# State stores issued earlier on the load queue, and the token sums of the multiplied-out MLP products moved from GpSimd to VectorE

## The chip, the cores and the metric

One core of a Trainium2 chip runs the whole program. The metric is the device time in microseconds of one execution; smaller is better. TensorE (PE) multiplies, ScalarE (ACT), VectorE (DVE) and GpSimd (POOL) work on what it needs and makes, and SyncE (SP) issues nearly all transfers from its queue.

## The reference

A two-layer decoder step for 512 prompt tokens and 32 sample tokens (544 columns), in float32, with 1024 features:

```python
for l in range(DEPTH):                       # DEPTH = 2
    h = rmsnorm(x, g_mix[l])
    if l < N_A_LAYERS:                       # layer 0: convolution module
        y, nh = conv_module(h, hist[l], w_pw1[l], b_pw1[l], w_dw[l], b_dw[l],
                            g_cln[l], b_cln[l], w_pw2[l], b_pw2[l])
        new_hist.append(nh)                  # the last 30 GLU rows: the "state"
    else:                                    # layer 1: latent attention
        q_lat, q_pe = mla_queries(h, cos, sin, w_dq[j], g_q[j], w_uq[j], w_qr[j], w_uk)
        ...
    x = x + y
    x = x + squared_relu_mlp(rmsnorm(x, g_ffn[l]), w_up[l], w_down[l])   # relu(h @ w_up)**2 @ w_down
```

The state of the prompt is 30 rows, that of each of the 8 sample sequences 30 rows.

## The kernel before

Features lie on the 128 partitions, tokens along the free dimension, so x is 8 chunks of 128x544. Each float32 factor is split into a high and a low part, and a product is three passes (high x high, low x high, high x low). A **unit** is one 128-column piece of a weight matrix: ACT copies its high part (`high`, line 679, tile wh), POOL subtracts to make its low part (`low`, line 524, tile wl), PE multiplies (`product`, line 1522, 48 matmuls of 272 columns in two halves). Two units come from one loaded **block** of 128x8x256 (1 MB, tile raw, line 466); there are two places for blocks, so the load of block n waits until the low parts of block n-2 are made. There are four half-places for weight parts, so the high part of unit u waits for the product of u-2, and two places in PSUM, so product u waits until DVE has read product u-2 (semaphore `freed`).

Every engine runs its own list in the order in which it is written; semaphores tie the lists together. The order around the change is:

- Second pointwise product of the convolution module: blocks 8 to 11 (`w_pw2`), 8 units. After each, `new_x` adds the product to x (DVE, line 1189), makes the next input's high part (ACT, line 687, xh), low part (DVE, line 1014, xl) and the square (ACT, line 693), and DVE adds it up (line 1026, acc). On ACT the call `ahead(u)`, which makes the high part of unit u+2, stands ahead of the rest of `new_x(u)`.
- The two state outputs, `o_convp` (from ext) and `o_convs` (from exs), are stored from the SP queue once the last gated rows are there (`u_out`). ACT waits for both stores (`s_out`) ahead of the MLP, since the MLP's tiles lie over ext and exs.
- MLP of a layer: 8 up products (`ML`), the first of which is followed by the matmuls of the column sums (`sums`, line 1532), ACT's square root (`root_of`, line 698) and DVE's `reciprocal` (line 1033). After it DVE applies the scale and the relu (`relu`, line 1200), ACT squares (`squared`, lines 786, 787), and DVE makes the low part (line 1012). In the same 8 steps the inputs of seven-factor products are prepared, in four groups k: ACT scales two chunks of x (`scaled_x`, line 776, bb), four subtractions make T1, T3, T2 and T4N (`token_sums`, lines 533 to 538, tt), ACT takes their high parts (`token_high`, line 780, th) and DVE their low parts (`token_low`, line 1213, tl). bb and tt have two places each.
- Then 12 pairs of an up block in seven factors (`factor`, line 1647) and a down block (line 1659), and the last down products.

Of the kernel before, what the change touches and what calls it, by code (L numbers as in the profile page):

```python
# [18 lines left out]
ALU = mybir.AluOpType  # L19
# [159 lines left out]
def decoder_program(nc, xT, hist, vecs, cons, rope_tab, rows0, page_table, cache_ckv, cache_kpe, w_pw1, w_pw2, w_up, w_down,  # L179
# [17 lines left out]
    with ExitStack() as ctx:  # L197
# [240 lines left out]
        def _(sp):  # L438
# [37 lines left out]
                         hist.rearrange("p c b t -> p (c b) t")).then_inc(s_hist, 16)  # L476
            sp.dma_start(pt[:, :], page_table).then_inc(s_idx, 16)
            sp.dma_start(r0[:, :], rows0).then_inc(s_idx, 16)
            for n in range(2, MB[0]):
                load(n)  # L480

            sp.wait_ge(u_out, 2 * DC)
            sp.dma_start(o_convp, ext[:, :, NP:NP + HIST]).then_inc(s_out, 16)
            sp.dma_start(o_convs.rearrange("p c b t -> p (c b) t"),
                         exs[:, :, :, NT:NT + HIST].rearrange("p c b t -> p (c b) t")).then_inc(s_out, 16)

            for n in range(MB[0], MB[0] + FB * DC - 2):
                load(n)

            sp.wait_ge(s_out, 32)  # L490
# [27 lines left out]
        def _(pool):  # L518
# [4 lines left out]
                pool.wait_ge(w_hi, u + 1)  # L523
                pf.tensor_tensor(weight(wl, u), weight_raw(u), f32(weight(wh, u)), ALU.subtract).then_inc(w_lo, 1)  # L524

            def token_sums(layer, k):

                n, i = layer * KH + k, k % 2
                pool.wait_ge(t_in, 2 * n + 2)
                if k >= 2:  # L530
                    pool.wait_ge(t_lo, n - 1)
                near, far = bb[:, i, 0, :], bb[:, i, 1, :]
                pf.tensor_tensor(tt[:, i, T1, :], near[:, TB], near[:, TA], ALU.subtract).then_inc(t_sum, 1)
                pf.tensor_tensor(tt[:, i, T3, :], far[:, TB], near[:, TB], ALU.subtract).then_inc(t_sum, 1)
                pool.wait_ge(t_sum, 4 * n + 1)
                pf.tensor_tensor(tt[:, i, T2, :], far[:, TB], tt[:, i, T1, :], ALU.subtract).then_inc(t_sum, 1)
                pool.wait_ge(t_sum, 4 * n + 3)
                pf.tensor_tensor(tt[:, i, T4N, :], far[:, TA], tt[:, i, T2, :], ALU.subtract).then_inc(t_sum, 1)

            def third_sum(layer, q):  # L540

                n = MB[layer] + DC // 2 + 2 * q
# [11 lines left out]

            def mlp(layer):
                for j in range(DC):
                    if 2 <= j < 2 + KH:
                        token_sums(layer, j - 2)
                    low(ML[layer] + j)
                third_sum(layer, 0)  # L560
                for q in range(PAIRS):
                    u = LU[layer] + q * PAIR
                    low(u)
                    low(u + 1)
                    fourth_sum(layer, q)
                    for j in range(2, PAIR):
                        low(u + j)
                    if q + 1 < PAIRS:
                        third_sum(layer, q + 1)
                for j in range(DC):  # L570
                    low(LD[layer] + j)
# [84 lines left out]
        def _(act):  # L656
# [39 lines left out]
            def root_of(dim, e=0, to=None):  # L696
                root_in()
                af.activation(halves(to or rstd[:, :]), SUMS, ACT.Sqrt, bias=eps[:, e:e + 1],
                              scale=1.0 / dim).then_inc(root, 1)
# [64 lines left out]

            for c in range(DC):
                new_x(U_PW2 + c, xh, "g_ffn0")
            root_of(D)

            def scaled_x(layer, g, k):

                n = layer * KH + k
                if k >= 2:
                    act.wait_ge(t_sum, 4 * (n - 1))
                for e in range(2):
                    c = k + e * KH
                    af.activation(bb[:, k % 2, e, :], x[:, c, :], ACT.Copy, scale=V(g, c)).then_inc(t_in, 1)

            def token_high(layer, k):
                act.wait_ge(t_sum, 4 * (layer * KH + k) + 4)
                af.activation(th[:, k, :, :], tt[:, k % 2, :, :], ACT.Copy).then_inc(t_hi, 1)  # L780
# [8 lines left out]
            def mlp(layer, g):  # L789
                for k in range(2):  # L790
                    scaled_x(layer, g, k)
                for j in range(DC):
                    ahead(ML[layer] + j)
                    squared(0, j)
                    if 1 <= j < 1 + KH:
                        token_high(layer, j - 1)
                    if 1 <= j < KH - 1:
                        scaled_x(layer, g, j + 1)
                for q in range(PAIRS):
                    u, n = LU[layer] + q * PAIR, layer * PAIRS + q  # L800
                    f, c = q // (DC // 2) + 1, q % (DC // 2) * 2

                    if n > 0:
                        act.wait_ge(u_read, n)
                    act.wait_ge(mm, u + 1)
                    af.activation(acc[:, TA], factor_out(u, 0), ACT.Copy).then_inc(u_copy, 1)
                    for j in range(FACTORS - 1):
                        ahead(u + j)
                    squared(f, c)
                    ahead(u + FACTORS - 1)  # L810
                    squared(f, c + 1)
                    for j in range(FACTORS, PAIR):
                        ahead(u + j)
# [167 lines left out]
            af.activation(mh[:, :, NP:T], ps[:, 5, 0:NH * NS].rearrange("p (h s) -> p h s", s=NS), ACT.Copy).then_inc(s_hi, 1)  # L981
            for c in range(DC):
                new_x(U_WO + c, xh2, "g_ffn1")
            root_of(D)
            mlp(1, "g_ffn1")
            for c in range(DC):
                u = LD[1] + c
# [8 lines left out]
        def _(dve):  # L996
# [33 lines left out]
            def reciprocal(to=None):  # L1030
                root_()
                r = to or rstd[:, :]
                link(df.reciprocal(r, r))
# [159 lines left out]

            for c in range(DC):
                new_x(U_PW2 + c, xl, xh, "g_ffn0", "b_pw2")
            reciprocal()

            def relu(dst, a, scale, sem_=None):

# [7 lines left out]
            def down(u, c):  # L1207
                dve.wait_ge(mm, u + 1)
                df.tensor_tensor(halves(x[:, c, :]), acc_of(u), halves(x[:, c, :]), ALU.add).then_inc(freed, 1)

            def token_low(layer, k):
                dve.wait_ge(t_hi, layer * KH + k + 1)
# [37 lines left out]
                squared_low(f, c)  # L1250

            def mlp(layer, nsrc):
                for j in range(DC):
                    u = ML[layer] + j
                    dve.wait_ge(mm, u + 1)
                    relu(halves((t0, t1)[j % 2][:, :]), acc_of(u), halves(rstd[:, :]), src)
                    dve.wait_ge(src, nsrc + j + 1)
                    dve.sem_inc(freed, 1)
                    squared_low(0, j)
                    if 2 <= j < 2 + KH:  # L1260
                        token_low(layer, j - 2)
                    if j == DC - 3:
                        first_sums(layer, 0)
                for q in range(PAIRS):
                    up_pair(layer, q, nsrc)
                    if q + 1 < PAIRS:
                        first_sums(layer, q + 1)
                    squared_low(q // (DC // 2) + 1, q % (DC // 2) * 2 + 1)
                    for j in range(2):
                        down(LU[layer] + q * PAIR + FACTORS + 2 * j + 1, q % (DC // 2) * 2 + j)  # L1270
# [212 lines left out]
            df.tensor_tensor(ml[:, :, NP:T], ps[:, 5, 0:NH * NS].rearrange("p (h s) -> p h s", s=NS), f32(mh[:, :, NP:T]), ALU.subtract).then_inc(s_lo, 1)  # L1483
            for c in range(DC):
                new_x(U_WO + c, xl2, xh2, "g_ffn1")
            reciprocal()
            mlp(1, FB * DC + 3 + NH // 2)
            for c in range(DC):
                u = LD[1] + c
# [499 lines left out]
```

## Time and profile before

| | us |
|---|---|
| median of three runs (lowest, highest) | 1467.7 (1467.69, 1469.43) |
| the profiled execution | 1465.78 |
| its span in the trace | 1464.0 |
| PE busy in the span | 1386.7 (95%) |
| DVE, ACT, POOL busy | 816.4, 606.9, 764.1 |
| mean granted TensorE clock | 0.979 of full |
| PE's share of the chain that ended last | 85% |
| share of `DMA raw<-w_up` in that chain | 2% |

Times within the trace are microseconds from the start of its span. The profiled execution lies 1.9 us under the median, so differences are taken in the trace and then applied to the median. A busy PE is no PE at its peak: matmuls overlap, so the distance from one product to the next is the measure.

### The profile page before, as it was taken

The page shows a single profiled execution, that of the slowest core. Times are in us where ns is not written, and L with a number is a line of the kernel's source. Part 1 is how long each engine was busy: PE and PEld are TensorE (multiplying, and loading weights), DVE is VectorE, ACT ScalarE, POOL GpSimd, SP SyncE. Part 2 cuts the span into 40 slices and gives each one's busy share as a digit, 9 for nine tenths or more (in the row PEclk, how much of TensorE's full clock was granted, in tenths as well). Part 3 has the DMA queues.
Part 4 walks back from the last instruction along what each step waited for, and adds up shares of the span by engine and source line. Part 5 has one row for each costly group of instructions (what it writes and reads, how often), then busy time and mean ns, then how long its engine had stood idle before and what let it go on. Part 6 is the DMA issues. An engine that isn't in the chain of part 4 may idle for free.

```text
span 1464.0 us, 28984 instructions
## 1 busy us (share of the span) xinstructions
PE 1386.7 (95%) x12444; PEld 1289.4 (88%) x12444; DVE 816.4 (56%) x1199; ACT 606.9 (41%) x1030; POOL 764.1 (52%) x541
## 2 busy tenths in 40 slices
PE   6999969799999999998899999999999999999995
PEld 5787759789999999998899967677998999999995
DVE  5658775455454454468456655655455545545435
ACT  5212243444444344345456644443354443444432
POOL 3422203468788888333323354340357887887732
PEclk9999979899999999999999999999999999999998
DMA  8312109323322322522111376662122322322221
GB/s 193 87 30 59 60 1 63 86 84 104 99 87 87 109 94 87 189 87 74 55 33 33 114 280 256 264 249 78 58 87 71 103 87 89 109 92 88 87 87 61
DMA packets 132143, 148.69 MB, mean 102 GB/s; under 512 B 22768, under 2 KB 123248, under 8 KB 127792
## 3 DMA queue, kind: packets, MB, share of 16 engines
q1 hardware_dynamic: 124848, 104.90, 25.3%
q0 software_dynamic: 7168, 41.95, 7.6%
q8 instruction: 98, 1.61, 0.5%
q14 instruction: 29, 0.24, 0.0%
HBM read 142.81 MB, written 4.03 MB: 100 GB/s over the span
## 4 chain that ended last, share of the span: by engine, by line
PE 85%; DVE 5%; POOL 3%; ACT 3%; DMA 2%; issue 1%; DVEq 0%; SPq 0%; ACTq 0%; POOLq 0%
PE ps L1522 27%; PE ps L1659 20%; PE ps L1647 17%; PE ps L1790 5%; PE ps L1564 3%; PE ps L1830 3%; POOL wl L524 2%; PE ps L1879 2%; DMA raw<-w_up 2%; ACT wh L679 1%; PE ps L1725 1%; PE ps L1860 1%; DVE xl L1014 1%; PE ps L1888 1%; PE ps L1584 0%
## 5 line engine op out<-in xcount | busy, mean ns | idle before, releaser
L524 POOL TENSOR_TENSOR wl<-raw,wh 128x512 fp32r<-128x512 f32 (+2 forms) x253 | 443.8, 1756 | 402.9 <-ACT wh L679 402.4
L679 ACT ACTIVATE wh<-raw 128x512 fp32r<-128x512 f32 (+2 forms) x253 | 192.6, 762 | 389.3 <-PE ps L1522 200.7
L524 POOL TENSOR_TENSOR wl<-wuv,wh 128x512 fp32r<-128x512 f32 x104 | 134.8, 1308 | 92.0 <-ACT wh L679 92.0
L1522 PE MATMUL ps<-xh,wh 128*128 128x272 f32 x704 | 152.6, 299 | 30.6 <-POOL wl L524 17.9
L1659 PE MATMUL ps<-mh,wh 128*128 128x272 f32 x768 | 158.6, 288 | 0.0
L1659 PE MATMUL ps<-mh,wl 128*128 128x272 f32 x768 | 158.6, 288 | 0.0
L1659 PE MATMUL ps<-ml,wh 128*128 128x272 f32 x768 | 158.3, 288 | 0.0
L1522 PEld LDWEIGHTS ps<-xh,wh 128*128 128x128 f32 x704 | 113.2, 194 | 42.8 <-POOL wl L524 31.0
L1522 PE MATMUL ps<-xl,wh 128*128 128x272 f32 x704 | 147.8, 292 | 0.0
L1522 PE MATMUL ps<-xh,wl 128*128 128x272 f32 x704 | 147.8, 293 | 0.0
L1659 PEld LDWEIGHTS ps<-ml,wh 128*128 128x128 f32 x768 | 120.4, 188 | 0.0
L1659 PEld LDWEIGHTS ps<-mh,wh 128*128 128x128 f32 x768 | 120.3, 188 | 0.0
L1659 PEld LDWEIGHTS ps<-mh,wl 128*128 128x128 f32 x768 | 119.9, 189 | 0.0
L1522 PE MATMUL ps<-mh,wh 128*128 128x272 f32 x544 | 113.6, 290 | 5.5 <-POOL wl L524 3.1
L679 ACT ACTIVATE wh<-wuv 128x512 fp32r<-128x512 f32 x104 | 65.4, 630 | 116.5 <-DVE wuv L1224 79.2
L1522 PEld LDWEIGHTS ps<-xl,wh 128*128 128x128 f32 x704 | 113.4, 193 | 0.0
L1522 PEld LDWEIGHTS ps<-xh,wl 128*128 128x128 f32 x704 | 112.9, 194 | 0.0
L1522 PE MATMUL ps<-mh,wl 128*128 128x272 f32 x544 | 112.8, 289 | 0.0
L1522 PE MATMUL ps<-ml,wh 128*128 128x272 f32 x544 | 112.7, 289 | 0.0
L1647 PE MATMUL ps<-th,wl 128*128 128x272 f32 x384 | 110.8, 289 | 0.0
L1647 PE MATMUL ps<-tl,wh 128*128 128x272 f32 x384 | 110.6, 288 | 0.0
L1647 PE MATMUL ps<-th,wh 128*128 128x272 f32 x384 | 110.6, 288 | 0.0
(284 smaller groups left out, 3080.2 us busy)
## 6 DMA issues: line engine op xcount, KB each, us to landing
raw<-w_up SPq DMA_DIRECT2D x32, 1024.0 KB, 5.4
raw<-w_down SPq DMA_DIRECT2D x32, 1024.0 KB, 5.1
raw<-w_pw SPq DMA_DIRECT2D x16, 512.0 KB, 5.1
raw<-w_pw SPq DMA_DIRECT2D x4, 1024.0 KB, 5.1
raw<-w_o SPq DMA_DIRECT2D x4, 1024.0 KB, 5.1
raw<-w_dq SPq DMA_DIRECT2D x3, 1024.0 KB, 5.3
raw<-w_uq SPq DMA_DIRECT2D x4, 768.0 KB, 4.4
x<-xT SPq DMA_DIRECT2D x4, 544.0 KB, 7.3
```

Of the source, the lines that this page charges most:

```text
L524: pf.tensor_tensor(weight(wl, u), weight_raw(u), f32(weight(wh, u)), ALU.subtract).then_inc(w_lo, 1)
L679: af.activation(weight(wh, u), weight_raw(u), ACT.Copy).then_inc(w_hi, 1)
L1014: df.scalar_tensor_tensor(dst, a, scale, f32(high), ALU.mult, ALU.subtract).then_inc(lo, 1)
L1522: m = tf.matmul(ps[:, 2 * (u % 2) + bank, 0:width], w[:, k, :], a[:, k, part], start=(k == 0 and n == 0), stop=(k == nk - 1 and n == 2))
L1564: m = tf.matmul(ps[SB * j:SB * (j + 1), conv_bank(c) + i, :], diag[part, c % 2, s + j, :], ext[part, c, s + j:s + j + NP], start=(s == 0), ...
L1647: m = tf.matmul(factor_out(u, i), w[:, k, :], part(a, k), start=(k == 0 and n == 0), stop=(k == KH - 1 and n == 2))
L1659: m = tf.matmul(acc_of(u)[:, h, :], w[:, k, :], a[:, k0 + k, h * HALF:(h + 1) * HALF], start=(k0 == 0 and k == 0 and n == 0), stop=(k0 > 0 ...
L1725: m = tf.matmul(out, k[:, c, j * P:(j + 1) * P], w[:, c, :], start=(c == 0 and m_ == 0), stop=(c == KC - 1 and m_ == 2))
L1790: m = tf.transpose(keys_at(n)[:, q * P:(q + 1) * P], a, ident)
L1830: m = tf.matmul(ps[NS * s:NS * (s + 1), 3 + i % 2, :], q, k, start=(c == 0), stop=(c == 2))
L1860: tf.matmul(out[:, c * NS:(c + 1) * NS], oc[:, (SPB * b + k) % SETS, cols], fold_w[:, b % 2, k, :], start=(k == 0), stop=False)
L1879: m = tf.matmul(ps[NS * s:NS * (s + 1), 6, 0:KL], pts[:, q, NS * s:NS * (s + 1)], latents(2 * i + s // 2)[:, r * KL:(r + 1) * KL], start=( ...
```

## The change

Three things are written differently. On SP, the two state stores stand ahead of the load of the third `w_pw2` block (number 10), and not behind the load of the last one (11). The subtractions of `token_sums` are on DVE and not on POOL: groups 0 and 1 ahead of the reciprocal, groups 2 and 3 at the end of steps 0 and 1. On ACT, `scaled_x` of groups 0 and 1 stands ahead of the square root, and `token_high` and the later `scaled_x` come one step sooner. This holds for the MLP of both layers.

```diff
-            for n in range(2, MB[0]):
-                load(n)
-
-            sp.wait_ge(u_out, 2 * DC)
-            sp.dma_start(o_convp, ext[:, :, NP:NP + HIST]).then_inc(s_out, 16)
-            sp.dma_start(o_convs.rearrange("p c b t -> p (c b) t"),
-                         exs[:, :, :, NT:NT + HIST].rearrange("p c b t -> p (c b) t")).then_inc(s_out, 16)
-
-            for n in range(MB[0], MB[0] + FB * DC - 2):
+            for n in range(2, MB[0] + FB * DC - 2):
+                if n == units[U_PW2].block + 2:
+                    sp.wait_ge(u_out, 2 * DC)
+                    sp.dma_start(o_convp, ext[:, :, NP:NP + HIST]).then_inc(s_out, 16)
+                    sp.dma_start(o_convs.rearrange("p c b t -> p (c b) t"),
+                                 exs[:, :, :, NT:NT + HIST].rearrange("p c b t -> p (c b) t")).then_inc(s_out, 16)
                 load(n)
...
             def mlp(layer):                                  # POOL
                 for j in range(DC):
-                    if 2 <= j < 2 + KH:
-                        token_sums(layer, j - 2)
                     low(ML[layer] + j)
...
             def mlp(layer, g):                               # ACT
                 for k in range(2):
                     scaled_x(layer, g, k)
+                root_of(D)
                 for j in range(DC):
                     ahead(ML[layer] + j)
                     squared(0, j)
-                    if 1 <= j < 1 + KH:
-                        token_high(layer, j - 1)
-                    if 1 <= j < KH - 1:
-                        scaled_x(layer, g, j + 1)
+                    if j < KH:
+                        token_high(layer, j)
+                    if j < KH - 2:
+                        scaled_x(layer, g, j + 2)
...
             def mlp(layer, nsrc):                            # DVE
+                for k in range(2):
+                    token_sums(layer, k)
+                reciprocal()
                 for j in range(DC):
                     u = ML[layer] + j
                     dve.wait_ge(mm, u + 1)
...
                     squared_low(0, j)
-                    if 2 <= j < 2 + KH:
-                        token_low(layer, j - 2)
+                    if j < KH:
+                        token_low(layer, j)
+                    if j < KH - 2:
+                        token_sums(layer, j + 2)
                     if j == DC - 3:
                         first_sums(layer, 0)
```

The calls `root_of(D)` and `reciprocal()` that stood behind the loop of `new_x` are gone from there. The four subtractions of a group are the same on DVE as they were on POOL.

The SP queue, from the loads of the second pointwise weights (w_pw 128x8x256) to the first up weights, before:

```order
L466 DMA raw<-w_pw 128x8x256 x4
L483 DMA o_convp<-ext 1024x1x30
L484 DMA o_convs<-exs 8192x1x30
L466 DMA raw<-w_up 128x8x256 x5
```

and in the change:

```order
L466 DMA raw<-w_pw 128x8x256 x2
L482 DMA o_convp<-ext 1024x1x30
L483 DMA o_convs<-exs 8192x1x30
L466 DMA raw<-w_pw 128x8x256 x2
L466 DMA raw<-w_up 128x8x256 x5
```

The stores have moved past two block loads. The larger one is 8192 pieces of 30 numbers (120 bytes).

DVE at the start of the MLP of layer 0, before, from the last sum of squares (acc) to step 2:

```order
L1026 TENSOR_TENSOR acc<-acc,sq 128x544
L1033 RECIPROCAL rstd<-rstd 128x544
L1200 SCALAR_TENSOR_TENSOR t<-ps,rstd 128x544
L1012 TENSOR_TENSOR ml<-sq,mh 128x544
L1200 SCALAR_TENSOR_TENSOR t<-ps,rstd 128x544
L1012 TENSOR_TENSOR ml<-sq,mh 128x544
L1200 SCALAR_TENSOR_TENSOR t<-ps,rstd 128x544
L1012 TENSOR_TENSOR ml<-sq,mh 128x544
L1213 TENSOR_TENSOR tl<-tt,th 128x1088
```

and in the change, where the relu is line 1179, group 0 of the sums stands first and group 1 (its last two rows are shown) next to the reciprocal:

```order
L1200 TENSOR_TENSOR tt<-bb,tt 128x272
L1202 TENSOR_TENSOR tt<-bb,tt 128x272
L1013 RECIPROCAL rstd<-rstd 128x544
L1179 SCALAR_TENSOR_TENSOR t<-ps,rstd 128x544
L992 TENSOR_TENSOR ml<-sq,mh 128x544
L1206 TENSOR_TENSOR tl<-tt,th 128x1088
L1197 TENSOR_TENSOR tt<-bb 128x272
L1198 TENSOR_TENSOR tt<-bb 128x272
L1200 TENSOR_TENSOR tt<-bb,tt 128x272
L1202 TENSOR_TENSOR tt<-bb,tt 128x272
L1179 SCALAR_TENSOR_TENSOR t<-ps,rstd 128x544
```

Between the relu of step 0 and that of step 1 there are now five more instructions; before there was only the low part of ml.

ACT at the same place, before:

```order
L698 ACT_TABLE_LOAD
L698 ACTIVATE rstd<-ps,eps 128x544
L776 ACTIVATE bb<-x,vec 128x544 x4
L679 ACTIVATE wh<-raw 128x1024
L786 ACTIVATE sq<-t 128x544
L787 ACTIVATE mh<-t 128x544
L679 ACTIVATE wh<-raw 128x1024
```

and in the change:

```order
L756 ACTIVATE bb<-x,vec 128x544 x4
L679 ACT_TABLE_LOAD
L679 ACTIVATE rstd<-ps,eps 128x544
L660 ACTIVATE wh<-raw 128x1024
L766 ACTIVATE sq<-t 128x544
L767 ACTIVATE mh<-t 128x544
L760 ACTIVATE th<-tt 128x1088
L756 ACTIVATE bb<-x,vec 128x544 x2
L660 ACTIVATE wh<-raw 128x1024
```

The four scalings stand ahead of the root, and a high part of sums and two scalings now stand between the squares of step 0 and the high part of the weights that step 1 makes.

## Rows read from the trace of the kernel before

**Rows 1.** Chain that ended last, layer 0: start us, us, what
```profile
239.64 24.39 DMA raw<-w_up
...
276.27 0.93 PE ps L1532 x4
...
300.83 25.57 PE ps L1522 x192
326.39 3.62 PE ps L1647 x29
```

**Rows 2.** The same chain, layer 1
```profile
1078.07 0.93 PE ps L1532 x4
...
1128.22 10.52 PE ps L1647 x84
```

**Rows 3.** Timeline of PE: start us, us, what [idle before <- releaser]
```profile
267.60 0.82 PE L1522 MATMUL ps<-xh,wh 128*128 128x272 f32 x2 [7.58 <-POOL wl L524]
...
284.79 0.51 PE L1522 MATMUL ps<-xh,wh 128*128 128x272 f32 x2 [1.61 <-POOL wl L524]
...
300.83 0.82 PE L1522 MATMUL ps<-xh,wh 128*128 128x272 f32 x2 [3.53 <-POOL wl L524]
...
665.22 0.62 PE L1522 MATMUL ps<-mh,wh 128*128 128x272 f32 x2 [1.88 <-DVE ml L1014]
...
694.51 0.52 PE L1522 MATMUL ps<-mh,wh 128*128 128x272 f32 x2 [1.77 <-POOL wl L524]
```

**Rows 4.** Timeline of the SP queue, three stretches
```profile
173.38 0.37 SPq L466 DMA_DIRECT2D raw<-w_pw  x1
...
227.92 1.54 SPq L484 DMA_DIRECT2D o_convs<-exs  x1
239.64 18.70 SPq L466 DMA_DIRECT2D raw<-w_up  x2
```

**Rows 5.** Transfers: issue, count, size, median us from issue to landing
```profile
raw<-w_up SPq DMA_DIRECT2D x32, 1024.0 KB, 5.4
...
o_convs<-exs SPq DMA_DIRECT2D x1, 960.0 KB, 32.6
```

**Rows 6.** Timeline of ACT
```profile
230.06 1.06 ACT L679 ACTIVATE wh<-raw 128x1024 fp32r<-128x1024 f32 x1 [3.35 <-PE ps L1522]
...
287.10 1.10 ACT L780 ACTIVATE th<-tt 128x1088 fp32r<-128x1088 f32 x1
288.10 1.38 ACT L776 ACTIVATE bb<-x,vec 128x544 f32<-128x544 f32 x2
```

**Rows 7.** Timeline of DVE
```profile
173.82 0.24 DVE L1062 SCALAR_TENSOR_TENSOR exs<-t,vec 128x32 f32<-128x32 f32 x1
...
249.90 2.32 DVE L1014 SCALAR_TENSOR_TENSOR xl<-x,vec,xh 128x544 fp32r<-128x544 f32 x1 [1.01 <-ACT xh L687]
252.15 0.71 DVE L1026 TENSOR_TENSOR acc<-acc,sq 128x544 f32<-128x544 f32 x1
254.12 0.78 DVE L1189 SCALAR_TENSOR_TENSOR x<-ps,vec,x 128x544 f32<-128x544 f32 x1 [1.26 <-PE ps L1522]
...
278.04 3.55 DVE L1033 RECIPROCAL rstd<-rstd 128x544 f32<-128x544 f32 x1 [3.97 <-ACT rstd L698]
...
285.24 0.71 DVE L1200 SCALAR_TENSOR_TENSOR t<-ps,rstd 128x544 f32<-128x544 f32 x1
...
293.95 1.29 DVE L1213 TENSOR_TENSOR tl<-tt,th 128x1088 fp32r<-128x1088 f32 x1
...
330.93 0.44 DVE L1235 TENSOR_TENSOR t<-ps,acc 128x272 f32<-128x272 f32 x1 [0.25 <-PE ps L1647]
```

**Rows 8.** Timeline of POOL
```profile
249.24 2.40 POOL L524 TENSOR_TENSOR wl<-raw,wh 128x1024 fp32r<-128x1024 f32 x1 [3.61 <-ACT wh L679]
```

**Rows 9.** Tile tt: engine op xcount: ns min/median/max, first and last start us
```profile
L533 POOL TENSOR_TENSOR tt<-bb x8: 773/782/1262, 279.3 to 1104.5; 128x272 f32<-128x272 f32 x8
```

**Rows 10.** Window 300.8 to 302: us, busy of PE, PEld, DVE, ACT, POOL; PEclk, DMA, GB/s
```profile
300.80:302.00 1.20, 1.17 (x5) 1.18 (x6) 1.20 (x2) 0.00 (x0) 0.00 (x0) 0.50 0.00 0
```

More of the change, by code:

```diff
@@ L524, in low @@
                 pf.tensor_tensor(weight(wl, u), weight_raw(u), f32(weight(wh, u)), ALU.subtract).then_inc(w_lo, 1)
[L526 to L538, printed above, removed]
             def third_sum(layer, q):
@@ L766, in _ @@
                 new_x(U_PW2 + c, xh, "g_ffn0")
-            root_of(D)
             def scaled_x(layer, g, k):
@@ L983, in _ @@
                 new_x(U_WO + c, xh2, "g_ffn1")
-            root_of(D)
             mlp(1, "g_ffn1")
@@ L1195, in _ @@
                 new_x(U_PW2 + c, xl, xh, "g_ffn0", "b_pw2")
-            reciprocal()
             def relu(dst, a, scale, sem_=None):
@@ L1209, in down, with token_sums @@
                 df.tensor_tensor(halves(x[:, c, :]), acc_of(u), halves(x[:, c, :]), ALU.add).then_inc(freed, 1)
+            def token_sums(layer, k):
+                n, i = layer * KH + k, k % 2
+                dve.wait_ge(t_in, 2 * n + 2)
+                if k >= 2:
+                    dve.wait_ge(t_lo, n - 1)
+                near, far = bb[:, i, 0, :], bb[:, i, 1, :]
+                df.tensor_tensor(tt[:, i, T1, :], near[:, TB], near[:, TA], ALU.subtract).then_inc(t_sum, 1)
+                df.tensor_tensor(tt[:, i, T3, :], far[:, TB], near[:, TB], ALU.subtract).then_inc(t_sum, 1)
+                dve.wait_ge(t_sum, 4 * n + 1)
+                df.tensor_tensor(tt[:, i, T2, :], far[:, TB], tt[:, i, T1, :], ALU.subtract).then_inc(t_sum, 1)
+                dve.wait_ge(t_sum, 4 * n + 3)
+                df.tensor_tensor(tt[:, i, T4N, :], far[:, TA], tt[:, i, T2, :], ALU.subtract).then_inc(t_sum, 1)
             def token_low(layer, k):
@@ L1485, in _ @@
                 new_x(U_WO + c, xl2, xh2, "g_ffn1")
-            reciprocal()
             mlp(1, FB * DC + 3 + NH // 2)
```

## The prediction

> **What bounds the kernel now.** I read the page first: PE is busy for 95% of the span and carries 85% of the chain that ended last, so a change pays only where PE stands still or runs at the lower clock, and everything behind such a place moves with it. Then I read the chain around the changed lines. In layer 0 its largest foreign piece is a transfer: the load of the first up block, issued at 239.64, on the chain for 24.39 us [rows 1]; the median load of that kind lands in 5.4 us [rows 5]. The SP queue shows why: the store of o_convs was issued at 227.92 [rows 4] and takes 32.6 us to land [rows 5], until 260.5, and the load stands behind it. PE waits 7.58 us, from 260.02 to 267.60 [rows 3]. It then starts at the lower clock, so that this product with the others up to the sums' matmuls (276.27, [rows 1]) takes 8.67 us, where a product at full clock is 6.0 to 6.05 us (x is written at 254.12 for the product before [rows 7], and PE is done with the next at 260.02 [rows 3]).
>
> The timeline of PE shows two more waits in each layer's up products, both for a low part that POOL made late: 1.61 and 3.53 us in layer 0 [rows 3]. At each of them POOL had one group of token sums in front of the weights' low part, 0.78 us for each of four subtractions [rows 9]. After the wait of 3.53 us the granted clock is 0.50 [rows 10], which is the 1.2 GHz level; the four products from 300.83 take 25.57 us [rows 1], 1.4 us over four at 6.05. Layer 1 is the same: from the sums' matmuls to the first factor 50.15 us [rows 2], against 50.12 in layer 0 [rows 1]. Nothing else in the span depends on the moved lines, so the sum is made from these two stretches.
>
> **Stores moved.** The gated rows of the last chunk are written at 173.82 + 0.24 = 174.1 [rows 7]. Before, the load of the third block was issued at 173.38 [rows 4]; now the stores go at 174.1 and the load right behind them, after their issuing (1.54 us for the large one [rows 4], of which the smaller one's is a part). With the landing of 32.6 us and then 5.4 us for the block behind it [rows 5], the third block is there at about 214. ACT first reads it at 230.06 [rows 6]: 16 us of cover. The stores are down by about 208, and ACT's wait for them stands at 262, so that costs nothing; if the cover were gone, each microsecond of lateness would cost one. The fourth block's load and the first up load are released by low parts that do not move, the latter at 239.64 [rows 4], and it now lands in 5.4 us, at 245. What is next in the line: ACT makes that unit's high part when the product before the last is done, 254.1, POOL its low part until 257.6 (2.40 us [rows 8]), both before PE is free at 260.02. Product one of the MLP starts at 260.07 and not at 267.60, at full clock: ends at 266.1 and not at 276.1. **Gain 10.0 us.** The last input chunk is no new stop: x is written at 260.1, its low part waits on POOL as at 249.90 (2.32 us, ends 4.1 us after x was written at 248.1, a product ahead of 254.12 [rows 7]), so it is there at 264.2, and PE comes to it at 265.3.
>
> **Token sums and the reciprocal.** I count from the sums' matmuls, S (276.27 and 1078.07 now; 266.3 in layer 0 then). The sum of squares ends 4.75 us behind the last x (252.86 less 248.1 [rows 7]), 264.85, S - 1.4 (by layer 1's trace about S - 1.1). A 128x272 subtraction on DVE is not in the trace with both inputs in SBUF. The nearest is 0.44 us with one input in PSUM [rows 7]; the bound from above is POOL's 0.78 [rows 9]; I take 0.43, and with starts that overlap 1.65 us a group. Two groups end at S + 1.9 to S + 2.2; the scalings they need (1.38 us a pair [rows 6]) are done at S - 1.2. The reciprocal now starts at S + 1.8 [rows 1, 7], so it starts 0.1 to 0.4 later, and the first relu, R, at S + 5.7 to S + 6.0, where it was S + 5.4. ACT's scalings ahead of the root fit into its wait. POOL's low part for product 2, with no sums before it, is ready at S + 5.2: product 1 after the sums ends at S + 6.85, product 2 starts at once. The wait of 1.61 us is gone, and the one of 3.53 us in that form.
>
> **What takes their place.** Step 0 now holds a chain. ACT: squares and high part of the sums, from R + 1.86 to R + 2.96 (285.24 to 287.10, 1.10 [rows 6, 7]), scalings to R + 4.24 [rows 6], then the high part of the weights for product 3 until R + 5.2 (1.06 [rows 6]). DVE: low part of the sums 1.29 [rows 7] to R + 4.3, then the four subtractions from R + 4.35. The third would end at R + 5.5; POOL, which asked at R + 5.25, starts its 2.40 us [rows 8] at R + 5.4, and the fourth waits. That DVE with two SBUF inputs stands still until POOL is done is what 249.90 shows: 2.32 us for an instruction that starts 0.66 us behind POOL's at 249.24 and ends 0.58 us after it [rows 7, 8]. So the fourth ends at R + 8.1, relu 1 at R + 8.75. PE has finished product 2 at S + 12.85 and can start product 3 at S + 14.55: a wait of 1.7 us. Step 1 repeats it: relu 2 starts 8.0 us after relu 1, product 4 starts 8.0 after product 3, a wait of 2.0 us. Groups 2 and 3 are then through; step 2 has no subtractions, and PE goes on without waits. The clock: after 1.77 us of waiting PE's first pair of matmuls took 0.52 us, as at full clock, after 1.88 us 0.62 us, a part of it at the lower [rows 3]. I take the lower clock once in a layer, with 1.4 us. From S: 14.55, +8.0, +6.05 +1.4, +3 x 6.05 = 48.1; with R at the early end 47.8. It was 50.1: **gain 2.3 us in layer 0, 2.0 to 2.3 in layer 1**, 4.6 together at the early end, which I take since layer 0's stretch lies there.
>
> The page "SBUF — State Buffer" of the Trainium skill, section "Who interferes with whom", says that a VectorE instruction with two SBUF inputs and a GpSimd instruction that reads SBUF exclude each other for a whole instruction; the trace agrees (2.32 us at 249.90). The page "GPSIMD Engine Reference" of the Trainium skill, section "Engine selection", would put elementwise work on VectorE as about twice as fast: by that alone the move saves and no wait comes back, which is the second case below; by the exclusion it costs two waits a layer.
>
> **Sum.** 10.0 + 4.6 = 14.6 us: span 1464.0 to 1449.4, the profiled execution 1465.8 to 1451.2, the median of 1467.7 to **1453.1**.
>
> **Rivals.**
> - The waits of step 0 and 1 come back without the lower clock, since 1.7 to 2.0 us lies about the 1.77 that did not bring it and the 1.88 that did: 2 x 1.4 less, 1450.3. Chance 0.20.
> - The fourth subtraction gets in ahead of POOL's low part. For: it is 0.04 us behind the third. Against: POOL asks 0.2 us earlier, and waits only for the one that runs. Then only product 3 waits (low part at R + 8.3, 1.3 us), at full clock; each layer ends 3.4 us sooner: 1446.3. If it also cost POOL nothing, 0.6 less in each layer: 1445.1. Chance 0.15.
> - A subtraction takes POOL's 0.78 us. The reciprocal is then 2.9 us later and each of two steps 1.4: 5.7 us a layer, 1464.5. Chance 0.03; in between (0.5 to 0.6 us, or one more lockout of 2.4 us in a step), 1455 to 1459, 0.08.
> - The stores do not hold the load: it would be late without them. For: other transfers share the queue. Against: 32.6 and 24.4 us end within 4 us of each other, and the 32 loads have a median of 5.4. Then 10.0 falls away: 1463.1. Chance 0.02.
> - Slower: the third block comes late. It stands behind 8192 small pieces; if these took 49 us and not 32.6 from 174 on, the block would miss 230.06, and each further microsecond costs one, first out of 14.6. The result turns at 64 us, about twice the row; three times the row, 98 us, gives 1453 + 49 = 1502. For: the stores now run while the convolution reads the same tiles. Against: on the old place they ran beside busy PE, DVE, ACT and POOL, and the products there kept their 6.0 us. Chance 0.03.
>
> **How the numbers follow.** My forecast holds 0.49. Its own range is 1451.5 to 1455. The range of all reaches to the second rival below and to the in-between case above, 1445.5 to 1457, and leaves out about 0.12. What a measurement tells from no change is 0.2%, 2.9 us. Faster by more 0.95, within 0.02, slower 0.03; only the last rival and half-way forms of the third and fourth are not faster.
>
> **What would show it.** In the changed trace the large store lands at about 208 and the first up load in 5 to 6 us; PE has no wait at 260; the sums' matmuls of layer 0 start near 266.3. The span from there to the first factor is 47.8 us in both layers, with two waits of PE of 1.3 to 2.0 us ahead of products 3 and 4, released by DVE's relu, and one of the four subtractions in each of groups 2 and 3 takes 2.4 us or more. The subtractions else take 0.43 us and the reciprocal starts right behind them. I am wrong if the third block's high part is later than 230.1, if DVE is locked out at another place, or if a stage behind takes the shift up.

## The result, and the profile after

| | before | changed |
|---|---|---|
| median, us (lowest to highest, 10 runs each) | 1467.7 (1464.86 to 1472.77) | 1459.8 (1457.2 to 1462.98) |
| ratio to before, 95% interval | | 0.9945 [0.9932, 0.9958] |
| span of the profiled execution, us | 1464.0 | 1458.0 |
| PE busy in the span, us | 1386.7 | 1386.7 |
| sums' matmuls start, layer 0 / layer 1, us | 276.27 / 1078.07 | 276.28 / 1074.49 |

The kernel is faster, by 7.9 us and not by the forecast 14.6: outside the range of 1445.5 to 1457. The last row of the table shows where the sum broke. The sums' matmuls of layer 0 should have come near 266.3, and came where they had been.

The chain that ended last in the changed kernel (start us, us, what), ahead of layer 0's MLP and in it:

```profile
183.00 2.13 PE ps L1561 x47
185.12 5.90 issue
191.02 6.55 PE ps L1561 x110
...
204.93 2.18 PE ps L1574 x4
...
234.12 36.36 PE ps L1519 x288
...
298.93 24.14 PE ps L1519 x192
```

Line 1561 is the depthwise taps, 1519 the product, 1574 the column means behind the taps, and "issue" is time in which PE waited for nothing that the profile shows. The up load that stood on the chain for 24.39 us [rows 1] is gone from it: from 234.12 PE multiplies for 36.36 us without a stop, over the place of the 7.58 us wait [rows 3]. In its place there are 5.90 us in the middle of the taps.

PE's timeline of the changed kernel (start us, us, what [idle before <- releaser]) shows that stop, and the two waits in the up products:

```profile
182.93 2.20 PE L1561 MATMUL ps<-ext,diag 32*32 32x512 f32 x47
191.02 6.43 PE L1561 MATMUL ps<-ext,diag 32*32 32x512 f32 x113 [5.90 <-issue]
...
276.28 1.08 PE L1529 MATMUL ps<-acc,con 128*128 128x272 f32 x4
...
290.95 0.49 PE L1519 MATMUL ps<-xh,wh 128*128 128x272 f32 x2 [1.63 <-DVEq L1254]
...
298.93 0.49 PE L1519 MATMUL ps<-xh,wh 128*128 128x272 f32 x2 [1.77 <-DVEq L1254]
```

The same run of 160 taps in PE's timeline of the kernel before, and the means behind it:

```profile
181.62 5.52 PE L1564 MATMUL ps<-ext,diag 32*32 32x512 f32 x160
...
194.50 2.18 PE L1577 MATMUL ps<-acc,invd 128*128 128x272 f32 x4 [4.76 <-DVEq L1151]
```

Before, the taps took 5.5 us from 181.62. Now they end at 197.45, 14.5 us after their start: 5.9 of stop, and 3.1 more because what follows ran at the lower clock. Two windows of the changed kernel (us, busy of PE, PEld, DVE, ACT, POOL; PEclk, DMA, GB/s) show both:

```profile
185.20:191.00 5.80, 0.00 (x0) 0.00 (x0) 0.85 (x2) 0.00 (x0) 0.00 (x0) 0.81 1.55 49
191.00:194.00 3.00, 2.98 (x61) 1.43 (x66) 0.00 (x0) 0.00 (x0) 0.00 (x0) 0.50 1.56 47
```

In the first every computing engine is all but idle, while the DMA engines show a share of 1.55 and move only 49 GB/s. In the second PEclk is 0.50, the 1.2 GHz level.

What runs there is the large store. The SP queue and the transfers of the changed kernel (issue, count, size, median us to landing), which answer to [rows 4, 5]:

```profile
175.40 0.62 SPq L482 DMA_DIRECT2D o_convp<-ext  x1
176.06 0.68 SPq L483 DMA_DIRECT2D o_convs<-exs  x1
176.78 60.88 SPq L466 DMA_DIRECT2D raw<-w_pw  x2
250.07 54.89 SPq L466 DMA_DIRECT2D raw<-w_up  x5
```

```profile
raw<-w_pw SPq DMA_DIRECT2D x1, 1024.0 KB, 29.7
o_convs<-exs SPq DMA_DIRECT2D x1, 960.0 KB, 28.4
```

The store is on its way from 176.06 to 204.5, over the whole last run of taps; before it began at 227.92 [rows 4], among products.

The page of the changed kernel counts PE's instructions and the packets of the queue q8, the only one with instruction packets of 16 KB (packets, MB, share of 16 engines):

```profile
PE 1386.7 (95%) x12444; PEld 1286.3 (88%) x12444; DVE 830.0 (57%) x1231; ACT 607.2 (42%) x1030; POOL 737.6 (51%) x509
q8 instruction: 98, 1.61, 0.5%
```

PE's 24888 matmuls and weight loads and its 382 recorded waits and drains make 98.7 times 256, for 98 packets. No other engine has as many instructions, so the packets are PE's. Around the stop there is one of them. The window 176.2 to 185.2 holds 4416 packets of q1 and none of q8; the window 185.3 to 185.5 reads:

```profile
q1 hardware_dynamic: 90, 0.01, 171.6%
q8 instruction: 1, 0.02, 79.2%
```

79.2% of 16 engines over 0.2 us is a packet of 2.5 us. It began when PE had already stopped, at 185.12, and PE went on 3.1 us after its end.

DVE's timeline in step 0 of the MLP, layer 0, changed kernel (compare [rows 7]), and POOL's row that collides with it:

```profile
278.44 3.54 DVE L1013 RECIPROCAL rstd<-rstd 128x544 f32<-128x544 f32 x1
...
285.02 1.29 DVE L1206 TENSOR_TENSOR tl<-tt,th 128x1088 fp32r<-128x1088 f32 x1 [0.28 <-ACT th L760]
286.41 0.44 DVE L1197 TENSOR_TENSOR tt<-bb 128x272 f32<-128x272 f32 x1
286.77 0.44 DVE L1198 TENSOR_TENSOR tt<-bb 128x272 f32<-128x272 f32 x1
287.12 0.44 DVE L1200 TENSOR_TENSOR tt<-bb,tt 128x272 f32<-128x272 f32 x1
287.60 2.52 DVE L1202 TENSOR_TENSOR tt<-bb,tt 128x272 f32<-128x272 f32 x1
290.03 0.71 DVE L1179 SCALAR_TENSOR_TENSOR t<-ps,rstd 128x544 f32<-128x544 f32 x1
```

```profile
287.29 2.52 POOL L521 TENSOR_TENSOR wl<-raw,wh 128x1024 fp32r<-128x1024 f32 x1 [5.76 <-ACT wh L660]
```

This is the forecast step by step: three subtractions of 0.44 us, the fourth locked out until POOL is done, the relu behind it, and PE released by that relu (line 1254). The four products from 298.93 take 24.14 us, where they took 25.57 [rows 1]. The clock did not fall; the window that answers to [rows 10] has a PEclk of 1.00:

```profile
298.93:302.00 3.07, 3.07 (x24) 3.07 (x25) 1.72 (x2) 2.99 (x4) 0.00 (x1) 1.00 0.02 5
```

**Account**, in the profiled executions. Up to the sums' matmuls of layer 0: 1.3 us later from the program's start (what stands ahead of the stores comes at 172.88 for 171.57, far ahead of any moved line), 9.1 us later from the last taps (both seen at the means, 194.50 and 204.93), 10.4 us earlier from there on because the up load is there in time: 276.27 stays 276.28. From there to the first factor 46.8 us in each layer (276.28 to 323.07, 1074.49 to 1121.29), for 50.12 and 50.15: 3.3 us gained twice. Between layer 0's first factor and layer 1's sums 0.3: 751.7 (1078.07 less 326.39 [rows 1, 2]) and 751.4. The last sums of squares are multiplied 1.0 us slower, at the lower clock. That makes 6.0, and the span is 6.0 us shorter.

### The profile page after: what moved, and what is told of

Same layout as the page of the kernel before. It is cut to its first block, busy times and chain, and to the rows that moved or that the text cites. A ratio compares the mean times of both kernels' runs of the same rounds, so it can differ in the third digit from the quotient of the medians.

```text
span 1458.0 us, 28984 instructions
## 1 busy us (share of the span) xinstructions
PE 1386.7 (95%) x12444; PEld 1286.3 (88%) x12444; DVE 830.0 (57%) x1231; ACT 607.2 (42%) x1030; POOL 737.6 (51%) x509
## 3 DMA queue, kind: packets, MB, share of 16 engines
q8 instruction: 98, 1.61, 0.5%
## 4 chain that ended last, share of the span: by engine, by line
PE 86%; DVE 8%; ACT 3%; issue 2%; POOL 1%; DMA 0%; DVEq 0%; SPq 0%; ACTq 0%
PE ps L1519 26%; PE ps L1656 20%; PE ps L1644 17%; PE ps L1787 5%; PE ps L1561 4%; PE ps L1827 3%; PE ps L1876 2%; POOL wl L521 1%; DVE rstd L1013 1%; ACT wh L660 1%; PE ps L1722 1%; PE ps L1581 1%; DVE xl L994 1%; DVE tt L1202 1%; PE ps L1885 1%
```

## Experiments

Times are medians; the ratio is to the kernel before on the same chip, with its 95% interval. Its medians were 1466.0 in the first group of runs, 1474.7 in the second and 1466.6 in the third, so groups are compared by their ratios.

**Each half alone.** stores_only is the kernel before with the changed SP list; sums_only is the changed kernel with the old SP list.

> Only the stores are moved; token sums stay on POOL. Theory 1 (PE's instructions come late while the many 120-byte pieces of the state store fill the transfer engines, and this bites in the convolution's tap matmuls, of which PE takes 30 in a microsecond): the stop of PE marked issue, 5.9 us at 185.1 in the changed kernel, is there, the wait of 7.6 us at 260 is gone; 10.0 gained, about 9.1 lost, so the time is 0 to 2 us under before, ratio 0.999. Theory 2 (the stop at 185 was an accident of the profiled execution, or comes from the new order of the MLP): no stop, 10 us gained, ratio 0.993.

> Only the token sums are moved; stores stay behind the last load of the second pointwise weights. If the two parts add up: no stop of PE at 185, the late load with its wait of 7.6 us is there as before, and the stretch from the sums' matmuls to the first factor is 46.6 to 48 us in both layers where it was 50.1: 2.3 to 3.5 us a layer, 5 to 7 us in all, ratio 0.9955. If the gain of the changed kernel came from the stores, ratio 1.000.

Measured: stores_only 1465.65 us, ratio 0.9997 [0.9987, 1.0007]; sums_only 1459.93 us, 0.9958 [0.9943, 0.9973]. The half that should have given 10.0 us gives nothing; the other gives 6.2 us by its ratio and has no stop in the taps, though PE waited 10.28 us for the late up load and not 7.58. PE's timeline of stores_only:

```profile
181.51 2.20 PE L1561 MATMUL ps<-ext,diag 32*32 32x512 f32 x47
191.44 6.94 PE L1561 MATMUL ps<-ext,diag 32*32 32x512 f32 x113 [7.73 <-issue]
```

So the stop belongs to the stores, whatever DVE and POOL do, and it comes behind the same 47th matmul.

**The stores after the taps.** Issued ahead of the fourth block instead, when the last taps are through:

```diff
-                if n == units[U_PW2].block + 2:
-                    sp.wait_ge(u_out, 2 * DC)
+                if n == units[U_PW2].block + 3:
+                    sp.wait_ge(conv_mm, DC)
```

> The changed kernel with the stores one load later (ahead of the fourth block) and waiting for the last tap matmuls (about 187). Theory 1 (late instructions): the store of 28 to 33 us runs while PE does the norm's few matmuls and then products of 0.125 us a matmul; no stop marked issue over 1 us, the taps end where they do before, the stores land by about 220, the fourth block is issued at 227 and lands at once, PE has no wait at 260: 9 us under the changed kernel, about 1451, ratio 0.989. Rival (any small-piece store before 228 takes PE's instructions away, wherever it runs): a stop of some us comes back between 188 and 222, and the gain over the changed kernel is under 4 us.

Measured: 1448.03 us, 0.9875 [0.986, 0.9891]. The taps in PE's timeline:

```profile
182.95 5.52 PE L1561 MATMUL ps<-ext,diag 32*32 32x512 f32 x160
```

The stop and the lower clock are gone, with the same store of the same pieces, which lands in 29.4 us. The sums' matmuls start at 267.12. Against sums_only the stores are now worth 0.83% of 1467.7, 12 us, give or take 3 by the two intervals; the estimate was 10.0. In the traces the sums' matmuls come 9.2 us earlier than before, 10.5 if counted from the start of the last taps (182.95 for 181.62). The price of the late load is itself not fixed: in sums_only the up load issued at 240.15 was on the chain for 27.74 us, in the kernel before for 24.39 [rows 1].

**What of the store does it?** The taps read ext while the stores read ext and exs, so a contended tile was a rival. stores_other_tile sends as many pieces of the same size from xh, which nothing writes at that time; stores_long_pieces sends the same 960 KB in 1024 pieces of 960 bytes. Both also take the small store from xh (line not shown). In both the state outputs hold other numbers, and ACT waits for the stores ahead of its first write of xh.

```diff
-                    sp.dma_start(o_convs.rearrange("p c b t -> p (c b) t"),
-                                 exs[:, :, :, NT:NT + HIST].rearrange("p c b t -> p (c b) t")).then_inc(s_out, 16)
+                    sp.dma_start(o_convs.rearrange("p c b t -> p (c b) t"),    # stores_other_tile
+                                 f32(xh[:, :, :]).rearrange("p c (b t) -> p (c b) t", t=34)[:, 0:DC * NB, 0:HIST]).then_inc(s_out, 16)
+                    sp.dma_start(o_convs.rearrange("p c b t -> p c (b t)"),    # stores_long_pieces
+                                 f32(xh[:, :, 0:NB * HIST])).then_inc(s_out, 16)
```

> The changed kernel, but the stores read the same number of 120-byte pieces from the tile xh, which nobody writes then, and not from ext and exs, so the state outputs hold other numbers; ACT waits for them ahead of the first write of xh. Theory 1 (late instructions): the stop of 5 to 7 us in the tap matmuls stays, time as the changed kernel, ratio 0.9945. Rival (the store and the tap matmuls read the same tile ext and hold each other up): no stop, 9 us faster, ratio 0.988.

> As the kernel that stores from tile xh at the changed place, with the same 960 KB for the large output in 1024 pieces of 960 bytes and not 8192 of 120 (the state outputs hold other numbers). Theory 1 in the form that the number of pieces is what crowds the transfer engines: the large store lands in 3 to 8 us, the stop of PE in the taps is gone or under 1 us, time 8 to 10 us under the changed kernel, ratio about 0.988. Rival (any transfer of this size behind the small prompt store holds PE's instructions up): the stop stays over 3 us, ratio 0.993 or more.

Measured: stores_other_tile 1457.81 us, 0.9951 [0.9935, 0.9966]; stores_long_pieces 1454.84 us, 0.9866 [0.9848, 0.9884]. PE's timeline of the first, then of the second:

```profile
192.65 6.07 PE L1562 MATMUL ps<-ext,diag 32*32 32x512 f32 x113 [7.00 <-issue]
```

```profile
185.18 4.33 PE L1562 MATMUL ps<-ext,diag 32*32 32x512 f32 x113 [1.51 <-issue]
```

The tile does not matter: the stop is as long from another. The pieces do: with an eighth of them the store lands in 8.7 us and the stop is 1.51 us, at the same place. Both are above what was expected (3 to 8 us, and under 1 us). The 1024 pieces of 120 bytes of the small store still ran there, and which of the two stores the 1.51 us belong to was not tested.

**The same pieces, few at a time.** stores_in_eight leaves the stores early in the program (behind the third block's load), still beside the taps, but as eight transfers of 1024 pieces, each issued when the one before it has landed.

```diff
-                if n == units[U_PW2].block + 2:
+                if n == units[U_PW2].block + 3:
...
-                    sp.dma_start(o_convs.rearrange("p c b t -> p (c b) t"),
-                                 exs[:, :, :, NT:NT + HIST].rearrange("p c b t -> p (c b) t")).then_inc(s_out, 16)
+                    for c in range(DC):
+                        if c > 0:
+                            sp.wait_ge(s_hist, 16 * (c + 1))
+                        sp.dma_start(o_convs[:, c, :, :], exs[:, c, :, NT:NT + HIST]).then_inc(s_hist if c < DC - 1 else s_out, 16)
```

> The changed kernel with the third block's load ahead of the stores, and the large store cut into 8 of 1024 pieces each (one feature chunk), each issued when the one before has landed (7 us each by the small store's landing, 174 to about 235), so that never more than 1024 or 2048 pieces are queued. Theory 1a (PE's 16 KB of instructions wait behind the pieces that are already queued): the stop in the taps shrinks to 0 to 2.5 us, ratio 0.987 to 0.989. Theory 1b (small pieces share the engines badly at any queue length): the stop stays 5 us or more, ratio 0.9945.

Measured: 1446.66 us, 0.9865 [0.985, 0.9879]. Its SP queue, its transfers and its taps:

```profile
176.72 40.06 SPq L486 DMA_DIRECT2D o_convs<-exs  x8
```

```profile
o_convs<-exs SPq DMA_DIRECT2D x8, 120.0 KB, 5.0
```

```profile
183.41 5.52 PE L1563 MATMUL ps<-ext,diag 32*32 32x512 f32 x160
```

The eight run beside the taps, from 176.7 on, and PE does not stop. So neither a store beside the taps nor its small pieces do it by themselves, but 8192 of them handed over at once. One thing else differs: the third block's load now goes ahead of the stores and not behind them. The next run takes it out of the question.

**A store among other taps.** If it is PE's supply, the stop must follow the store, and the products must stay free of it. extra_store_mid is stores_after_taps with one more store of 8192 pieces, from xh at 91.34, ahead of an earlier run of taps; the later stores wait for it and overwrite what it writes.

```diff
...
+                if n == 7:
+                    sp.dma_start(o_convs.rearrange("p c b t -> p (c b) t"),
+                                 f32(xh[:, :, :]).rearrange("p c (b t) -> p (c b) t", t=34)[:, 0:DC * NB, 0:HIST]).then_inc(s_hist, 16)
```

> The kernel with the stores behind the last taps, and one more store of 8192 pieces of 120 bytes (from xh into the same output, overwritten later), issued at about 90 us, so that it runs beside products (92 to 107) and the taps of chunk 4 (107 to 115). Theory 1 (PE runs out of instructions in taps): no stop in the products, a stop marked issue of 2 to 8 us in the taps at 107 to 115 or just behind, ratio 3 to 9 us above the kernel with the stores behind the taps. Rival (the stop belongs to the last chunk, its ext data or its place in the program): no stop over 1 us there, time equal to that kernel's 1448.

Measured: 1468.88 us, 0.9958 [0.9943, 0.9973], 0.8% above stores_after_taps by the ratios of their two groups. That is 12 us, where 3 to 9 were expected: the stops are 8.25 us together, and the last taps start 14.15 us later than in stores_after_taps (197.10 for 182.95), since PE also ran at the lower clock behind each stop. PE's timeline in the first run of 224 taps:

```profile
108.44 2.26 PE L1565 MATMUL ps<-ext,diag 32*32 32x512 f32 x54
114.41 6.03 PE L1565 MATMUL ps<-ext,diag 32*32 32x512 f32 x128 [3.70 <-issue]
124.99 3.90 PE L1565 MATMUL ps<-ext,diag 32*32 32x512 f32 x42 [4.55 <-issue]
...
197.10 5.53 PE L1565 MATMUL ps<-ext,diag 32*32 32x512 f32 x160
```

Two windows of it, with the counts of matmuls and weight loads:

```profile
114.30:124.90 10.60, 6.03 (x128) 2.47 (x128) 3.45 (x5) 0.00 (x0) 0.00 (x0) 0.83 0.97 106
124.90:197.05 72.15, 70.87 (x1098) 53.36 (x1098) 47.86 (x67) 16.22 (x23) 19.44 (x9) 0.95 0.15 46
```

The first stop begins at 110.7. The store went out at 91.34 and the next block's load only at 112.12, so no load stood behind the store then.

These rows name the mechanism. The two stops are 128 matmuls and 128 weight loads apart, 256 instructions. From the second stop to the place behind the 47th tap of the last run are 1098 + 47 matmuls and as many loads, 2290 instructions, and the stored trace has 14 waits of PE between them, which the views do not count: 2304, nine times 256. The stops lie on one grid of 256 of PE's own instructions. The page "Runtime: NRT & Kernel Launch" of the Trainium skill, section "Instruction fetch mechanics", says that an engine's instructions are refilled in blocks of 256, 16 KiB, through a DMA queue, and that the cost of crossing from one to the next is "mostly hidden". The trace agrees with the block (98 packets, 1.61 MB in the whole span); that it is hidden does not hold beside 8192 small pieces.

The stored traces give the time of each packet and of each of PE's instructions. Counted with its waits, the instruction behind the 47th tap is number 5057, and number 4801, 256 ahead of it, stands in the run of taps before. A number on the grid is called a border here. The last two runs of the table are shown further below.

| | PE passes 4801, us | q8 packet starts | and takes | PE goes on with 5057 |
|---|---|---|---|---|
| before | 176.27 | 177.49 | 1.05 | 182.84, no stop |
| stores_in_eight | 178.06 | 180.79 | 1.30 | 184.63, no stop |
| stores_long_pieces | 176.13 | 182.73 | 0.96 | 185.18 |
| changed | 177.58 | 185.37 | 2.54 | 191.02 |
| stores_other_tile | 178.12 | 187.98 | 2.72 | 192.65 |
| stores_only | 176.16 | 187.09 | 2.07 | 191.44 |
| sums_behind_relu | 176.04 | 188.55 | 2.78 | 193.56 |
| changed_again | 176.53 | 189.13 | 2.50 | 194.07 |

Without the store beside the taps the packet starts 1.2 to 1.5 us after PE has passed the border before (before, sums_only, stores_after_taps, best and best_again), and PE has its instructions in time. Beside 8192 pieces it starts 7.8 to 12.6 us after, takes twice as long, and PE goes on 2 to 3.1 us behind its end. The later the packet, the longer the stop. In extra_store_mid PE passes the border before the first stop at 98.76, among products, and the packet starts at 109.41.

The same happens at the store's old place, among products. Number 6081, four blocks on, is reached there while the store runs. In the kernel before, PE passed 5825 at 239.82, the packet started at 248.93 and ended at 252.18, and PE came to 6081 at 255.73. In sums_only the packet ended at 253.65, and PE's timeline has a stop at that very instruction:

```profile
256.89 0.52 PE L1522 MATMUL ps<-mh,wl 128*128 128x272 f32 x2 [0.37 <-issue]
```

**The subtractions behind the relu.** sums_behind_relu is the changed kernel, with the subtractions of groups 2 and 3 moved behind the relu of the step after:

```diff
                     dve.sem_inc(freed, 1)
+                    if 1 <= j < KH - 1:
+                        token_sums(layer, j + 1)
                     squared_low(0, j)
                     if j < KH:
                         token_low(layer, j)
-                    if j < KH - 2:
-                        token_sums(layer, j + 2)
```

best has the stores after the taps as well.

> The changed kernel, with the subtractions of groups 2 and 3 on DVE behind the next step's relu and not ahead of it. If PE's waits of 1.63 and 1.77 us ahead of products 3 and 4 come from the relu queued behind the four subtractions and the lockout: relu 1 starts 4.3 us behind relu 0 and not 8.0, PE waits at most 0.7 us ahead of product 3 (for POOL's low part, which ACT starts late) and not at all ahead of product 4; the stretch is 43.9 us and not 46.6 in both layers, 5.4 us together, ratio 0.991. Rival (the low part of the weights is as late as the relu and holds PE by itself): 1 us a layer or less.

> Both later places together: stores behind the last taps, subtractions of groups 2 and 3 behind the relu. If the two do not touch each other: 10 us for the stores and 5.4 us for the subtractions under the changed kernel, 1443 on the scale where before is 1466, ratio 0.984.

Measured: sums_behind_relu 1461.17 us, 0.9895 [0.9873, 0.9918], in spite of a stop of 9.98 us in its taps; best 1449.37 us, 0.9826 [0.9811, 0.9841]. PE's only wait in layer 0's up products of best, then DVE's timeline:

```profile
280.88 0.52 PE L1519 MATMUL ps<-xh,wh 128*128 128x272 f32 x2 [0.59 <-POOL wl L521]
```

```profile
277.19 0.72 DVE L1179 SCALAR_TENSOR_TENSOR t<-ps,rstd 128x544 f32<-128x544 f32 x1
278.13 0.44 DVE L1197 TENSOR_TENSOR tt<-bb 128x272 f32<-128x272 f32 x1 [0.22 <-DVE t L1179]
278.49 2.63 DVE L1198 TENSOR_TENSOR tt<-bb 128x272 f32<-128x272 f32 x1
```

A subtraction is still locked out for 2.63 us, and it costs nothing there: what PE waits for is the relu, which now stands ahead of it. From the sums' matmuls to the first factor it is 43.78 us in layer 0 (267.25 to 311.03) and 43.80 in layer 1, 3.0 less than with the change; 0.49% by the ratios of best and stores_after_taps, 7 us, agrees with twice 3.0 as far as the intervals allow.

**Both again, side by side.**

> The changed kernel as it is, for a comparison on the same chip: ratio 0.9945; stop of 5 to 10 us in the taps.

> Stores behind the last taps and subtractions behind the relu, beside the changed kernel on the same chip: ratio 0.983 to before, that is 10 + 5.4 = 15 to 17 us under the changed kernel.

Measured: changed_again 1457.48 us, 0.993 [0.9916, 0.9945]; best_again 1438.51 us, 0.9819 [0.9806, 0.9831]. best is 1.7% and 1.8% faster than the kernel before. In changed_again PE's taps read:

```profile
194.07 6.11 PE L1561 MATMUL ps<-ext,diag 32*32 32x512 f32 x113 [9.98 <-issue]
```

The place of the stop is fixed, its length is not: 5.90, 7.73, 7.00, 9.98 and 9.98 us in the traces of changed, stores_only, stores_other_tile, sums_behind_relu and changed_again. It goes with the start of the packet in the table above.

## Why the prediction was right and wrong

**Stores moved: the step that failed is its cost of nothing.** The prediction said that "The stores are down by about 208, and ACT's wait for them stands at 262, so that costs nothing". The store did land, at 204.5; the third block at 206.5 (176.78 + 29.7) was 24 us ahead of 230.06; the up load came in time; the wait at 260 and its lower clock vanished. All that was right, and its 10.0 us turned up in stores_after_taps, as 12 by the ratios and 10.5 in the traces. But I asked only who waits for the store's data and for the loads behind it. The stop is in PE's own supply of instructions, for which no semaphore waits: the packet that brought the next 256 started 7.8 us after PE had passed number 4801, where it was 1.2 us. Neither the order of the lists nor any row of before shows this at that place. It cost 5.9 us and then 3.1 at the lower clock, out of 10.0.

**The evidence read too widely.** Against the slow rival stood that in the old place the stores "ran beside busy PE, DVE, ACT and POOL, and the products there kept their 6.0 us". The products did, but not because the store left PE's instructions alone. In a product 48 matmuls take 6.0 us, so PE needs some 16 us for 256 instructions (15.9 from 5825 to 6081); in the taps 160 matmuls take 5.52 us [the row of before above], so 256 instructions last 4.4 us, and 6.6 from 4801 to 5057 with the wait between the two runs. With the store, the time from one border to the next was 13.4 us in the changed kernel, 15.3 in stores_only, 17.5 in changed_again, 15.7 and 10.6 in extra_store_mid and, among products, 16.6 in sums_only. So a block came every 10.6 to 17.5 us there: far more than the taps give, and about what products give. That before had no stop among its products was partly luck: its packet ended 3.5 us ahead of PE, and PE went on up to 3.1 us behind a packet's end elsewhere. The row that would have warned is the pace of the instructions at the new place.

**The rival of the late third block** named a collision in the right stretch, but with the wrong victim: it had 24 us of cover left.

**Token sums: right in its mechanism, small in its size.** Durations 0.44 us (forecast 0.43), lockout 2.52 us (2.4 or more), waits 1.63 and 1.77 us in layer 0 and 1.63 and 1.76 in layer 1 (1.7 and 2.0), the reciprocal at S + 2.2 (at S + 1.8 before: 0.4 later, the late end). The term mis-sized was the clock: no lower clock came after 1.77 us, so "I take the lower clock once in a layer, with 1.4 us" was wrong, and the first rival was right, with 0.20. With S to the first factor 46.8 for 47.8, the two layers gave 6.7 and not 4.6; 1.0 went at the lower clock of the last sums of squares, where no changed line stands. That the relu was queued behind the lockout, and not the lockout itself, was nearly the whole of PE's loss is what best shows: of 1.63 and 1.77 us of waiting 0.59 are left, for POOL's low part.

**Sum.** Forecast 10.0 + 4.6. Measured in the trace: 10.4 - 9.1 for the stores, 6.7 for the sums, 0.3 between the layers, -1.3 at the program's start and -1.0 at its end: 6.0, and a median 7.9 lower. The 1.3, 0.3 and 1.0 lie where no line was moved, and I don't count them as the change's; what the median has beyond the one trace I can't divide.

**Open.** The fetch starts late and not only runs slowly, but why it starts late, and by anything from 7.8 to 12.6 us, no row says: the stored trace has when a packet starts, not when it was asked for. The number and the size of the pieces were only changed together. VectorE and ScalarE were late there too in two traces: in changed_again VectorE starts its copy at 202.88, 2.7 us after the last tap, where it is 0.2 us in the changed kernel, and in sums_behind_relu PE waits 2.41 us for ScalarE's copy, where it is 1.53 in stores_only. Why is open. Spans also differ between kernels in layer 1's gathers, by 4 to 7 us without a changed line there (177.6 us for that stage in stores_after_taps and sums_only, 184.6 in best), so a difference of a few us between two single traces says nothing without its place.

## What to carry over

Before moving a transfer of many small pieces, look at what PE executes at its new place: a stretch of short matmuls uses up instructions several times faster than a product, and is starved of them where the product just gets through; give the pieces out in parts, make them longer, or wait until the stretch is over. Where VectorE and GpSimd can lock each other out, order the list so that what TensorE waits for stands ahead of the instruction that can be locked out. When a wait is removed and the end does not move, compare the start of each stage ahead of it too: here the loss lay 70 us before the gain.

## What the runs showed of the hardware

- TensorE stopped for 5.9 to 10 us in its taps beside a store of 8192 pieces of 120 bytes, and for 3.7 and 4.55 us in an earlier run of taps, on a grid of 256 of its instructions; beside 1024 pieces of 960 bytes together with the small store for 1.51 us; beside eight chained transfers of 1024 pieces of 120 bytes not at all. Among products it stopped for 0.37 us in one trace and not in another.
- The packet with TensorE's next 256 instructions started 1.2 to 1.5 us after the border before without the store (0.9 to 1.2 us long), and 7.8 to 12.6 us after it beside the store (2.1 to 2.8 us long), in the last run of taps.
- The 960 KB landed in 28.4 us as 8192 pieces and in 8.7 us as 1024; a 1 MB load issued behind the first took 29.7 us, where the median is 5.4 [rows 5].
- After waits of 1.63, 1.76 and 1.77 us the granted clock of TensorE stayed at the 2.4 GHz level; after the stop of 5.90 us it was at 1.2 GHz.
